# Memory attention's output projection as plain f32 products, and two expert weight chunks loaded earlier

## The reference, cut to what matters

```
def cross_attn(h, k, v, w_mq, w_mo):
    q = (h @ w_mq).reshape(B, L, MEM_HEADS, MEM_HD)
    s = jnp.einsum('blhd,bmhd->bhlm', q, k).astype(jnp.float32) * (MEM_HD ** -0.5)
    p = jax.nn.softmax(s, axis=-1).astype(v.dtype)
    o = jnp.einsum('bhlm,bmhd->blhd', p, v).reshape(B, L, D)
    return o @ w_mo
...
x = x + cross_attn(rmsnorm(x, norm_mem_q), mk, mv, w_mq, w_mo)
x = x + moe(rmsnorm(x, norm_moe), w_router, b_router, w_up, b_up, w_down, b_down)
```

## Time and profile before

| | before |
|---|---|
| median of 3 runs | 1231.01 us (1230.34 to 1236.89) |
| the profiled execution | 1230.39 us, its span 1228.6 us |
| TensorE busy | 1173.3 us (95% of the span) |
| VectorE, ScalarE busy | 407.4 us, 302.8 us |
| read from HBM | 438.06 MB, 360 GB/s over the span |
| mean granted TensorE clock | 0.985 |

### The profile page before, as it was taken

One profiled execution on the slowest core, in us unless ns is written; L12 is line 12 of the kernel. 1 busy time (PEld: TensorE's weight loads), 2 busy tenths in 40 slices (PEclk: granted clock), 3 DMA queues, 4 the chain that ended last, 5 costly groups with the idle time before them and its releaser, 6 DMA issues.

```text
span 1228.6 us, 14737 instructions
## 1 busy us (share of the span) xinstructions
PE 1173.3 (95%) x5768; PEld 562.0 (46%) x5768; DVE 407.4 (33%) x722; ACT 302.8 (25%) x491; POOL 36.5 (3%) x90
## 2 busy tenths in 40 slices
PE   6999999997999999999999999899989989989995
PEld 3788869894333333333333333233333333323332
DVE  3543766723223131333223131313313222222224
ACT  5454244423111112221111112122111111111113
POOL 2001600000000000000000000000000000000000
PEclk9999999998999999999999999899999999989998
DMA  8650416377999999999999999999999999999994
GB/s 299 240 210 1 156 36 198 145 317 303 382 385 429 429 428 428 428 428 429 428 428 429 428 429 428 428 429 429 428 428 428 429 429 428 428 426 429 427 428 161
DMA packets 49986, 442.28 MB, mean 360 GB/s; under 512 B 3931, under 2 KB 16803, under 8 KB 25216
## 3 DMA queue, kind: packets, MB, share of 16 engines
q1 hardware_dynamic: 40464, 316.94, 62.5%
q10 hardware_dynamic: 8432, 121.66, 23.3%
q0 software_dynamic: 1056, 3.21, 0.7%
HBM read 438.06 MB, written 3.73 MB: 360 GB/s over the span
## 4 chain that ended last, share of the span: by engine, by line
PE 94%; DVE 2%; another core or an unknown queue 1%; issue 1%; ACT 0%; POOL 0%; DVEq 0%; ACTq 0%; POOLq 0%
PE ps L456 38%; PE ps L470 18%; PE ps L339 15%; PE ps L433 7%; PE ps L463 3%; PE ps L477 2%; PE ps L478 2%; PE ps L439 2%; PE ps L448 1%; PE ps L1788 1%; PE ps L1599 1%; PE ps L1573 1%; PE ps L1745 1%; PE ps L1804 1%
## 5 line engine op out<-in xcount | busy, mean ns | idle before, releaser
L456 PE MATMUL ps<-regionB,regionP 128*64 128x512 f32 x1024 | 241.3, 614 | 10.6 <-DMA regionB<-in_w_up 10.6
L456 PE MATMUL ps<-regionA,regionP 128*64 128x512 f32 x1024 | 225.9, 598 | 5.7 <-DMA regionA<-in_w_up 4.9
L470 PE MATMUL ps<-regionD,regionP 128*64 128x512 f32 x992 | 225.0, 595 | 0.0
L749 DVE TENSOR_TENSOR regionP<-ps,regionP 128x512 f32<-128x512 f32 x32 | 22.1, 691 | 401.9 <-PE ps L439 401.9
L456 PEld LDWEIGHTS ps<-regionA,regionP 128*64 128x64 f32 x1024 | 72.1, 138 | 148.1 <-issue 138.0
L456 PEld LDWEIGHTS ps<-regionB,regionP 128*64 128x64 f32 x1024 | 69.6, 140 | 145.7 <-issue 132.9
L470 PEld LDWEIGHTS ps<-regionD,regionP 128*64 128x64 f32 x992 | 68.3, 137 | 129.1 <-issue 128.9
L743 DVE SCALAR_TENSOR_TENSOR roundedP<-regionP,roundedP 64x512 fp32r<-64x512 f32 x62 | 43.8, 746 | 158.5 <-ACT roundedP L627 158.5
L642 ACT ACTIVATE regionP<-ps 128x512 f32<-128x512 f32 x31 | 18.5, 597 | 298.1 <-PE ps L433 298.1
L433 PE MATMUL ps<-regionP 128*64 128x512 f32 x384 | 90.4, 607 | 1.2 <-DVE regionP L709 1.2
L783 DVE TENSOR_TENSOR regionP<-ps,regionP 128x1024 f32<-128x1024 f32 (+1 forms) x48 | 58.5, 1219 | 95.7 <-PE ps L478 85.1
(11 more groups left out here) (302 smaller groups left out, 1162.7 us busy)
## 6 DMA issues: line engine op xcount, KB each, us to landing
regionA<-in_w_up SPq DMA_DIRECT2D x64, 2048.0 KB, 41.8
regionB<-in_w_up SPq DMA_DIRECT2D x64, 2048.0 KB, 43.6
regionD<-in_w_down ACTq DMA_DIRECT2D x58, 2048.0 KB, 14.8
regionA<-in_w_in SPq DMA_DIRECT2D x4, 2048.0 KB, 14.0
regionD<-in_w_down SPq DMA_DIRECT2D x4, 2048.0 KB, 15.1
regionB<-in_w_mk SPq DMA_DIRECT2D x4, 1024.0 KB, 9.2
regionD<-in_w_mv SPq DMA_DIRECT2D x4, 1024.0 KB, 21.2
regionD<-in_w_out SPq DMA_DIRECT2D x4, 1024.0 KB, 12.6
```

The lines of the kernel that those rows point to most:

```text
L456: ins = pe.matmul(ps[64 * half:64 * half + 64, n_, :], XTe[:, k % 4, k // 4, :], w[:, k, 1024 * half + 512 * n_:1024 * half + 512 * n_ + 512],
L470: ins = pe.matmul(ps[64 * n_:64 * n_ + 64, at_bank, :], rows[:, k, :], w[:, k, 512 * n_:512 * n_ + 512], start=(k == 0), stop=(k == KT - 1))
```

## The change

The tiles of `mo0` to `mo7` are multiplied whole, in f32, straight from the loaded `w_mo` and from one unsplit copy `ao` of the attention's result. The splitting of `w_mo` and of that result is gone. `PV0` to `PV4` are freed by ScalarE's copy. Chunks 0 and 3 of expert 0's `w_up` are loaded behind chunk 2, after the query projection; before, they came behind `mo3` and `mo7`.

```diff
-    t += [(f"PV{i}", "D") for i in range(5)]
+    t += [(f"PV{i}", "A") for i in range(5)]
...
-        aoH, aoL = gxH, catH
+        ao = reg(GX_at, 2560).rearrange("p (k t) -> p k t", k=KT)
...
             load_up0(2)
+            load_up0(0)
+            sp.wait_ge(filled, J.filled_at("mq7"))
+            load_up0(3)
             has(sp, "PV4")
...
             has(sp, "mo3")
-            load_up0(0)
             load_down0(0)
-            has(sp, "mo7")
-            load_up0(3)
             sp.wait_ge(filled, J.filled_at("router"))
             load_up0(1)
             load_down0(1)
...
-            for g in range(7, 10):
-                high_square(g)
+            high_square(7)
...
-            high_square(10)
-            high_square(11)
             for h in range(4):
                 took(act, f"PV{h}")
-                act.activation(aoH[:, 2 * h:2 * h + 2, 0:LP], bank(f"PV{h}").rearrange("p (d l) -> p d l", d=2),
-                               ACT.Copy).then_inc(S("aoH"), 1)
+                free(act.activation(ao[:, 2 * h:2 * h + 2, 0:LP], bank(f"PV{h}").rearrange("p (d l) -> p d l", d=2),
+                                    ACT.Copy), f"PV{h}")
             took(act, "PV4")
-            act.activation(aoH[:, :, LP:NT], bank("PV4").rearrange("p (d l) -> p d l", d=KT), ACT.Copy).then_inc(S("aoH"), 1)
+            free(act.activation(ao[:, :, LP:NT], bank("PV4").rearrange("p (d l) -> p d l", d=KT), ACT.Copy), "PV4")
...
-                if k in (1, 4, 7):
-                    low_square(7 + k // 3)
+                if k == 1:
+                    low_square(7)
...
-            low_square(10)
-            low_square(11)
-            for h in range(4):
-                dve.wait_ge(S("aoH"), h + 1)
-                free(dve.tensor_tensor(aoL[:, 2 * h:2 * h + 2, 0:LP],
-                                       bank(f"PV{h}").rearrange("p (d l) -> p d l", d=2), aoH[:, 2 * h:2 * h + 2, 0:LP].bitcast(F32),
-                                       ALU.subtract), f"PV{h}")
-            dve.wait_ge(S("aoH"), 5)
-            free(dve.tensor_tensor(aoL[:, :, LP:NT], bank("PV4").rearrange("p (d l) -> p d l", d=KT),
-                                   aoH[:, :, LP:NT].bitcast(F32), ALU.subtract), "PV4")
+            took(dve, "PV4")
...
             for k in range(KT):
-                pe.wait_ge(S("wsqL"), 9 + k // 2)
+                pe.wait_ge(S(f"wsq_in{k // 2}"), 48)
                 begin(f"mo{k}")
+                def whole(js):
+                    for j in js:
+                        ins = pe.matmul(bank(f"mo{k}", NT), wsq[:, k // 2, j, 128 * (k % 2):128 * (k % 2) + 128], ao[:, j, :],
+                                        start=(j == 0), stop=(j == KT - 1))
+                    return ins
                 if k < 7:
-                    end(square("mo", k, 8 + k // 2, (aoH, aoL), range(KT), 0))
+                    end(whole(range(KT)))
```

More of the change, by code:

```diff
@@ L1156, in high_square @@
                 if g >= 4:
-                    took(act, f"{('out', 'mq', 'mo')[g // 4 - 1]}{2 * (g % 4) + 1}")
+                    took(act, f"out{2 * (g % 4) + 1}")
                 high(act, wsqH[g % 4][:, 0:rows], wsq[:, g % 4, 0:rows]).then_inc(S("wsqH"), 1)
@@ L1830, in _ @@
                     continue
-                square("mo", k, 8 + k // 2, (aoH, aoL), range(4), 0)
+                whole(range(4))
                 has(pe, "mo6")
@@ L1837, in _ @@
                     pe.matmul(part[j % 3], gwr[:, j, :], xT[:, j, :], start=(j < 3), stop=(j in (4, 5)))
-                end(square("mo", k, 8 + k // 2, (aoH, aoL), range(4, KT), 0))
+                end(whole(range(4, KT)))
             pe.wait_ge(S("sqsum2"), 6)
```

## The result

The changed kernel takes 1236.6 us in the median of 12 runs (1234.33 to 1239.71), the kernel before 1231.1 us in 12 (1229.06 to 1236.89). The ratio is 1.0036 with a 95% interval of 1.0021 to 1.0052: 0.36% slower, 4.4 us (2.6 to 6.4); the two medians themselves lie 5.5 us apart, inside that interval. The profiled execution took 1237.63 us, its span is 1235.8 us, 7.2 longer than before.

What follows compares the result with a forecast made beforehand. The weight stream bounds the experts, its end set by TensorE's first expert chunk. Terms 6.3 - 0.7 - 1.6 = +4.0 us on a median of 1231.0 gave 1235.0 us, range 1232.0 to 1238.5.

Steps and rivals of the forecast that it cites:

- What sets the end: Whole kernel: what moves TensorE's first expert chunk moves the end by as much; bytes arriving before 303 us gain nothing.
- the step that was forecast: Experts: TensorE takes 55.1 us to a pair up to its first wait for weights, whose loads take 58.7 us.
- The products, +6.3: Attention's output projection, mo0 to mo7: 64 plain tiles at 0.538 us take 6.3 us more than three rounded products each.
- The rival at the price of four rounded products to a tile: Output projection: a plain tile costs 0.586 us, the stage 9.4 us more; the dearer-tile rival including this had 6%.
- The handoff, -0.7: Between PV4 and mo0: ScalarE's copy alone releases TensorE, without VectorE's subtraction, 0.7 us less.
- The splitting, zero: Weight copies leaving ScalarE and subtractions leaving VectorE: zero gain, bounded by 0.65 us.
- The clock, -1.6: At mo0: with TensorE idle 0.7 us instead of 1.41, the clock likely stays up, 1.6 us less.
- the sum of zero: At the gather: low clock comes at another time, up to 2.5 us less or about 1 more; taken as nothing.
- The loads, zero: Expert 0's w_up chunks 0 and 3 loaded earlier: they only widen a hole in the transfers, zero.
- The sum: Whole kernel: products, handoff and clock together give +4.0 us, a median of 1235.0 us, 0.3% slower.

Runs made afterwards that it cites:

- loads late: Changed kernel with all four chunks of expert 0's w_up issued only at the router's result; ratio to the kernel before 1.0064.
- idle time back: Changed kernel with mo0 held back until VectorE has prepared the router's weights, so TensorE again idles about 1.4 us before it; ratio to the kernel before 1.0056.
- half the tiles: Changed kernel with every second tile of the attention's output projection left out (32 of 64); ratio to the kernel before 0.9904.
- the split products in the same order: Kernel before, split products kept, with PV4 computed third; ratios 0.9971 and 0.9981. Compared with the changed kernel in that order, ratios 1.0053 and 1.0037.

## Why the prediction was right

**What sets the end.** Right, and shown twice: the last length stayed at 900.4 to 901.2 us in ten profiles of twelve while the part with the change moved between 67.1 and 84.8 us; of the other two, one has its loads late (903.67 us), and one lost 2.4 us on TensorE late (idle time back, 902.95). And half the tiles moved the end by what they moved TensorE.

Both would look the same if TensorE alone paced the kernel to its end. That the weights do is in the page of the changed kernel, where TensorE stands idle for them late in the experts:

```profile
L456 PE MATMUL ps<-regionB,regionP 128*64 128x512 f32 x1024 | 238.4, 608 | 11.7 <-DMA regionB<-in_w_up 11.7
```

Up to there TensorE keeps the step that was forecast: its reloads of the first chunk follow every 55.1 us from 366.63 to 752.55 us. And the time from the first reload to the last weights' arrival, read to a quarter of a microsecond, is 901.0 to 901.3 us in the eight profiles with the clock up behind that reload and the loads landed, and 904.5 us with the loads late.

**The products, +6.3.** Right. Stage, step (0.271 and 0.269 us a record) and record count (128) are as read from L1745. Against the split products in the same order the stage is 6.1 us longer. The rival at the price of four rounded products to a tile, 0.586 us, did not come: the 64 tiles took 0.54 each, 3.7 rounded products of 0.1465. The Trainium skill, page "FP8 and Floating Point Precision", section "TensorE Precision Notes", gives a true FP32 product four passes. If it is four, one takes 0.1345 us, an estimate from that page's count and the 0.538; the trace shows two records to a tile, and no run here counts passes.

**The handoff, -0.7.** Right: 0.69 us idle instead of 1.41.

**The splitting, zero.** Right: from the scores to `mo0` it is 25.99 us and was 26.71, and the handoff's 0.7 is all of that difference.

**The clock, -1.6.** Right, and the link to the idle time at this place is shown as far as the runs go: ahead of `mo0`, with 1.41 to 1.50 us idle it fell in three profiles of three, with 0.69 us or none in none of nine. Its price varied, 1.6 to 2.9 us. But the length of the idle time alone does not decide. Ahead of L1745 TensorE stands idle 1.36 us and the clock fell in none of the twelve profiles. And the stretch near 176 us begins within 1 us behind the next gap, ahead of 336 rounded products; this gap all twelve profiles have, with 1.34 or 1.35 us, but only five the stretch. Here it is in the first profile of before, which lacks it:

```profile
175.33 0.41 PE L339 MATMUL ps<-roundedP,roundedA 128*128 128x320 f32 x1 [1.34 <-DVE regionP L1423]
```

What else it takes is open; the prediction named the narrow products of 64 columns ahead of the gap, and no run took them away while keeping the gap. At the gather it fell in every profile; there the sum of zero held: from the stage's end to the first reload it is 20.26 us in the changed kernel's first profile and 20.37 before. Over all profiles its 12 records took 4.29 to 5.39 us.

**The loads, zero.** Right; the size of the later holes, which decides from where late loads would cost, was not in the prediction, and in the later expectation it was half of what it is. The first reload was forecast near 310.3 us and came at 313.37, or 310.2 without the 3.2 us ahead of the scores.

**The sum.** 4.0 was forecast, 3.9 is in the profiles and 4.4 in the ratio. That it meets the first pair of profiles to 0.1 us is partly luck: against the second profile of before it is 3.6, because there the clock's fall at `mo0` cost 2.9 us and the gather's 0.9 less. The median to expect, 1235.0 us, was 1.6 below the measured 1236.6. What it left out is the low stretches ahead of the changed part; the changed kernel's profiles reach the scores 3.2 and 3.9 us later than the first of before, which has none. Low stretches go with the spread of the timed runs as well: in the changed kernel's second timing the two runs with a mean clock of 0.985 took 1238.4 and 1238.5 us, and the one with 0.990 took 1233.3 us. With 5 to 8 us between the runs of one kernel, a median over three is a weak base.

## What to carry to other kernels

Count the records of an instruction against the code before its mean is used as a price: here a plain f32 matmul is two records and costs as much as 3.7 rounded ones, so replacing a three-part product by a plain one costs time on TensorE, and the end here moved with TensorE, though it frees the two engines that the end does not wait for. Ask of an earlier load which hole in the transfers it fills; if another hole lies between it and the point from which the stream is continuous, it is worth nothing. And an idle time of 1.4 us ahead of a dense stage can cost more in clock than in waiting (1.6 to 2.9 us here at `mo0`), though it does not at every place: look at the granted clock behind each gap. Filling this one by a change of order was worth some 3 us and made the better kernel.

## What was not expected of the hardware

The clock's low stretches appear at different places in executions of the same program: near 44 us in two profiles of the changed kernel and in none of the other ten, near 176 us in five, at `mo0` in the three with the long idle time, near 325 us in three, and at the gather in all. From 730 us on, where TensorE waits for weights, and behind its last product every profile has more of them. Up to 400 us a stretch lasted some 3 to 8 us and cost up to half its length: 1.4 us near 176, some 2.9 near 44, up to 3.2 near 325. That is most of what two executions of one kernel differ by in these profiles. The same gap can bring one or not: behind 1.34 us of idle time 336 rounded products took 49.6 to 49.8 us in seven profiles and 51.1 us in five.
